# Two transformer blocks on one core: four of nine modulation groups summed on VectorE beside the input projections

## The chip, the core and the metric

The kernel runs on one NeuronCore of one Trainium2 chip. The core's engines have a queue of instructions each and wait for one another by semaphores: TensorE (PE; its weight loads are PEld) multiplies matrices into eight PSUM banks, VectorE (DVE) and ScalarE (ACT) read PSUM and on-chip memory, GpSimd (POOL) on-chip memory alone, and SyncE (SP) issues the transfers from main memory, which 16 engines carry out. The metric is the time of one execution on the device, in microseconds.

## The reference

The input is one sequence of 256 tokens of width 1024, in float32. The first block has two layers (l = 0 "even", l = 1 "odd"), the second block one more. What matters here is the modulation, a product of one vector with a wide matrix for each layer, which does not depend on the tokens:

```python
cs = silu(c)                                   # (1, 1024)
for l in range(2):
    mod = (cs @ ada_w[l] + ada_b[l])           # 1024 -> 6 x 1024
    sh1, sc1, g1, sh2, sc2, g2 = split(mod, 6)
    h = rms_norm(x, norm1_g[l]) * (1 + sc1) + sh1
    y = mixer_l(h, ...)                        # h @ w_in, rope, attention, @ w_out
    x = x + g1 * y
    h = rms_norm(x, norm2_g[l]) * (1 + sc2) + sh2
    x = x + g2 * hier_moe(h, ...)
```

The even mixer projects h to 3072 columns and has eight plain heads and four differential ones; the odd mixer projects to 2608 columns (five tiles of 512 and a tail of 48) and has 16 heads with two softmax branches and a third over compressed keys. Sixteen routed experts follow each.

## The kernel before, in words

**Weights.** All weights go through a ring of six slots (`ring`), each a tile of 1024 x 512 float32 (2 MB, 128 partitions x 8 chunks x 512). SP loads the tiles in the one order of the table `PHASES`; tile n goes into slot n mod 6 once TensorE has counted tile n - 6 as used (`tile_used`). An engine that reads a tile waits for `landed` of its slot.

**Modulation.** The vector of 2048 numbers of a group G is four tiles. Groups 0 to 2 belong to layer 0, 3 to 5 to layer 1 and 6 to 8 to the second block: 0, 3 and 6 hold shift and scale ahead of a mixer or an expert stage that has to wait for them, and 1, 2, 4, 5 are wanted only later (gate 1, shift 2, scale 2, gate 2). `mod_tile` takes a tile in 32 matmuls: for each of 8 chunks and 4 quarters q of the columns the stationary operand is one column of `cact` spread over 32 columns, and the moving one the 128 columns of the weight; the result is on rows 32 q of a bank. A float32 matmul leaves two records in the trace, so a tile is 64. ScalarE copies the bank (`mod_out`), TensorE turns it in four transposes (`mod_turn`), and VectorE adds the bias and makes 1 + scale (`mod_columns`), which raises `mod_ready`.

**Where it stood.** Groups 1, 2 (layer 0) and 4, 5 (layer 1) were spread over the steps of the attentions `att0` and `att1` by `mod_chunk_steps`: a tile per step in `att0`, a third of a tile per step in `att1`. Their bank 2 and copy in `hT` are free there.

**Attention.** `att0` has eight items, `att1` 24 (eight rounds of two plain items and a compressed one). In step t TensorE makes the scores of item t in banks 6 and 7 (L2178, L2180), then modulation, P times V of item t - 1 - lag (L2202), and the transposes of P of item t - lag (L2227). VectorE in step t copies its half of the turned P (L543), makes the masked maximum of the scores of t (L1334), and normalises item t - 1 by the sums of the exponentials (L1344 to L1363); ScalarE copies its half, makes the exponentials of t (L931) and copies an output out (L938). lag is 1 in `att0` and 2 in `att1`. Scores of t + 1 wait for the maximum of t.

**Input projections.** `project` takes a weight tile in 2 x 8 matmuls of 128x512 (L2117), a row of tokens after another, into two of the four banks 0 to 3. Between the halves stand transposes of q and k by groups (`BETWEEN`; L2072), which alternate between banks 4 and 5: group g waits until g - 2 has been copied out, even ones by ScalarE (L1092), odd ones by VectorE (L1801). VectorE's and ScalarE's loops over the tiles j first copy the groups up to the first half of tile j, then tile j's result to `pb`. GpSimd applies the rope in between. In layer 1 VectorE makes, after the groups of j = 4, eight adds (L1845) for the compressed keys, which the matmuls of L2751 need.

## Time and profile before

| | us |
|---|---|
| median of 3 runs | 1359.21 (1359.13 to 1361.91) |
| profiled execution | 1359.62, its span 1357.9 |
| TensorE busy, share of the span | 1232.0, 91% |
| VectorE busy | 444.3, 33% |
| ScalarE, GpSimd busy | 267.6 and 115.8 |
| moved from main memory | 355.14 MB, 262 GB/s over the span |
| L2135, the modulation's matmuls, all nine groups | 82.1 in 2304 records |

The span's start is zero in all views. A stretch's line gives each engine's busy time in it; busy times count a pipelined matmul to its modelled end, so that those of neighbours overlap by some 0.1 us. PEclk is the clock that TensorE was granted as a share of 2.4 GHz; 0.50 is its lower level of 1.2 GHz. What stands in brackets after an instruction is its engine's idle time before it and who ended it. The first input projection runs from 36 to 125 us, `att0` to 163, the second projection from 357 to 433, `att1` from 456 to 533.

### The profile page before, as it was taken

Reading aid. Unit: us, or ns where it says so; the run is one execution under the profiler, and the core shown is the slowest. Engines: PE = TensorE matmul, PEld = TensorE weight load, DVE = VectorE, ACT = ScalarE, POOL = GpSimd, SP = SyncE. Lnnn points to the kernel's source line nnn. Section 1 sums busy time; section 2 is a strip of 40 time slices with the busy share of each in tenths; the row PEclk is TensorE's granted clock in tenths of the full one; section 3 lists DMA queues with packets and bytes.
Section 4 is the critical chain, followed back from the end, with each engine's and each line's share of the span. In section 5 each row is a group of like instructions: output and inputs, shape, how many; then the busy total and the mean of one; then the engine's idle time right before and its main releaser. Section 6 shows DMA issues by size and latency. Waiting matters only on the chain.

```text
span 1357.9 us, 17790 instructions
## 1 busy us (share of the span) xinstructions
PE 1232.0 (91%) x7440; PEld 649.5 (48%) x7440; DVE 444.3 (33%) x1148; ACT 267.6 (20%) x621; POOL 115.8 (9%) x202
## 2 busy tenths in 40 slices
PE   4999987999799899799999999899999599999895
PEld 4445743435445665344448845555545343333332
DVE  1102643113203574421153642431132731201124
ACT  0102511122101354212112122002320311020010
POOL 1010010000011000100001000000000222222221
PEclk9899997999999799989999999999999799999998
DMA  9956964999983565469999533383326579999993
GB/s 355 369 177 205 368 202 141 348 373 387 384 291 124 205 233 184 139 211 348 380 386 387 210 124 124 124 300 136 114 101 216 218 253 362 382 387 387 386 385 122
DMA packets 222955, 357.43 MB, mean 263 GB/s; under 512 B 15845, under 2 KB 86038, under 8 KB 222870
## 3 DMA queue, kind: packets, MB, share of 16 engines
q1 hardware_dynamic: 209056, 352.33, 73.6%
q10 hardware_dynamic: 13814, 3.87, 1.3%
q8 instruction: 64, 1.05, 0.3%
q14 instruction: 21, 0.17, 0.0%
HBM read 355.14 MB, written 1.05 MB: 262 GB/s over the span
## 4 chain that ended last, share of the span: by engine, by line
PE 82%; DVE 7%; DMA 4%; ACT 3%; issue 2%; SPq 1%; POOL 0%; DVEq 0%; ACTq 0%
PE bank L2117 20%; PE bank L2318 8%; PE bank L2524 8%; PE bank L2367 4%; PE bank L2810 4%; PE bank L2210 4%; PE bank L2135 4%; DMA ring<-in_w_down 3%; PE bank L2859 3%; PE bank L2293 3%; PE bank L2596 2%; PE bank L2387 2%; PE bank L2202 2%; PE bank L2227 1%; PE bank L2475 1%
## 5 line engine op out<-in xcount | busy, mean ns | idle before, releaser
L2117 PE MATMUL bank<-ring,hT 128*128 128x512 f32 x416 | 183.8, 601 | 3.3 <-ACT hT L895 2.4
L2117 PEld LDWEIGHTS bank<-ring,hT 128*128 128x128 f32 x416 | 79.2, 193 | 99.4 <-issue 98.6
L2524 PE MATMUL bank<-ring,A 128*64 128x512 f32 x512 | 116.5, 601 | 1.8 <-DVE pb L1722 1.8
L2318 PE MATMUL bank<-ring,A 128*64 128x512 f32 x512 | 117.2, 603 | 0.0
L2135 PE MATMUL bank<-ring,cact 128*32 128x128 f32 x2304 | 82.1, 297 | 18.0 <-issue 10.4
L2117 PE MATMUL bank<-ring,OT 128*128 128x512 f32 x224 | 97.2, 593 | 1.3 <-ACT OT L1212 0.8
L751 POOL TENSOR_TENSOR rstd<-rstd,nhalf 128x1 f32<-128x1 f32 x20 | 17.2, 859 | 810.2 <-DVE rstd L1281 810.2
L2135 PEld LDWEIGHTS bank<-ring,cact 128*32 128x32 f32 x2304 | 68.3, 119 | 33.4 <-issue 25.8
L2524 PEld LDWEIGHTS bank<-ring,A 128*64 128x64 f32 x512 | 35.1, 138 | 72.2 <-issue 70.7
L2117 PEld LDWEIGHTS bank<-ring,OT 128*128 128x128 f32 x224 | 42.2, 190 | 53.5 <-issue 52.5
L2318 PEld LDWEIGHTS bank<-ring,A 128*64 128x64 f32 x512 | 34.5, 138 | 66.6 <-issue 66.6
L2367 PE MATMUL bank<-ring,pb 128*64 128x512 f32 x256 | 57.0, 595 | 0.0
L2210 PE MATMUL bank<-ring,hT 128*128 128x512 f32 x128 | 55.8, 594 | 0.0
L2810 PE MATMUL bank<-hT,ring 128*128 128x256 f32 x256 | 55.8, 380 | 0.0
L2810 PEld LDWEIGHTS bank<-hT,ring 128*128 128x128 f32 x256 | 48.5, 190 | 6.7 <-issue 0.2
L2859 PE MATMUL bank<-ring,hT 128*128 128x512 f32 x96 | 42.2, 592 | 0.0
L2210 PEld LDWEIGHTS bank<-ring,hT 128*128 128x128 f32 x128 | 24.2, 190 | 29.1 <-issue 29.0
L543 DVE COPY PT<-bank 128x384 f32<-128x384 f32 (+1 forms) x34 | 17.7, 522 | 53.2 <-PE bank L2227 51.0
L1525 DVE TENSOR_TENSOR A_parts<-bank,OT_parts 128x512 fp32r<-128x512 f32 x32 | 22.1, 692 | 36.7 <-ACT OT_parts L1005 36.7
L2367 PEld LDWEIGHTS bank<-ring,pb 128*64 128x64 f32 x256 | 17.6, 137 | 34.5 <-issue 31.6
L2596 PE MATMUL bank<-ring,pb 128*64 128x512 f32 x128 | 29.0, 598 | 4.7 <-DMA ring<-in_w_down 4.7
L2293 PE MATMUL bank<-pb_parts 128*128 128x512 f32 x64 | 29.1, 455 | 3.7 <-DVE pb_parts L1458 3.7
(470 smaller groups left out, 1663.5 us busy)
## 6 DMA issues: line engine op xcount, KB each, us to landing
ring<-in_ada_w SPq DMA_DIRECT2D x24, 2048.0 KB, 10.1
ring<-in_moe_w_gate SPq DMA_DIRECT2D x32, 1024.0 KB, 8.0
ring<-in_moe_w_up SPq DMA_DIRECT2D x32, 1024.0 KB, 10.6
ring<-in_moe_w_down SPq DMA_DIRECT2D x16, 2048.0 KB, 19.7
ring<-in_w_gate SPq DMA_DIRECT2D x16, 2048.0 KB, 11.6
ring<-in_w_up SPq DMA_DIRECT2D x16, 2048.0 KB, 11.0
ring<-in_w_down SPq DMA_DIRECT2D x16, 2048.0 KB, 20.1
ring<-in_w_in SPq DMA_DIRECT2D x13, 2048.0 KB, 19.6
```

Of the source, the lines that this page charges most:

```text
L2117: ins = mm(B[2 * (m % 2) + tt][:], lhs[:, c, tt * P:(tt + 1) * P], w[:, c, :], start=c == 0, stop=c == C - 1)
L2135: ins = mm(B[MOD_RAW_BANK[G]][32 * q:32 * (q + 1), k * P:(k + 1) * P], cact[:, c0 + c:c0 + c + 1].broadcast_to([P, 32]), w[:, c, q * P:(q ...
L2202: ins = mm(dst, lhs, rhs, start=start, stop=stop)
L2210: ins = mm(B[2 + tt][:], hT[:, c, tt * P:(tt + 1) * P], w[:, c, :], start=c == 0, stop=c == C - 1)
L2293: ins = mm(bank[:], part[:, tt, c * P:(c + 1) * P], wide_sel[:, tt, 512 * half:512 * (half + 1)], start=tt + l == 0, stop=tt + l == 2)
L2318: ins = mm(B[r][64 * b:64 * (b + 1), :], wide_h[c][:, slot:slot + 64], w[:, 2 * r + b, :], start=c == 0, stop=c == C - 1)
L2367: ins = mm(B[r][64 * b:64 * (b + 1), :], hidT_small[half][k][:, slot:slot + 64], w[:, 2 * r + b, :], start=k == 0, stop=k == 1)
L2387: ins = mm(B[5 - j + tt][:], wT[NR * half + r][:, P * tt:P * (tt + 1)], part[r], start=half + r + l == 0, stop=half == 1 and r + l == NR)
L2524: ins = mm(B[r][64 * b:64 * (b + 1), :], wide_h[c][:, slot:slot + 64], w[:, 2 * r + b, :], start=c == 0, stop=c == C - 1)
L2596: ins = mm(B[r][64 * b:64 * (b + 1), :], hidT_wide[half][k][:, slot:slot + 64], w[:, 2 * r + b, :], start=k == 0, stop=k == 3)
L2810: ins = mm(B[2 * (m % 2) + a // 2][:, (a % 2) * T:(a % 2 + 1) * T], w[:, c, a * P:(a + 1) * P], hT[:, c, :], start=c == 0, stop=c == C - 1)
L2859: ins = mm(B[4 + q % 2][:], hT[:, c, (q % 2) * P:(q % 2 + 1) * P], w[:, c, :], start=c == 0, stop=c == C - 1)
```

## The change

Tiles of groups 1, 2, 4 and 5 are loaded between the tiles of the input projection of their layer. VectorE multiplies each chunk of such a tile by its column of `cact` and adds the eight up in half of `tmp` (`mod_sum`: one multiply, seven multiply-adds of 128x512); TensorE multiplies the sum with a stationary operand of 32 columns of ones, four matmuls in place of 32, behind the matmuls of a projection tile (`mod_summed_tile`). Copy, turn and columns move to the projection too, through banks 6 and 7 and the buffer `PT`. The attention's steps hold none of it any more. The tiles of the compression, `cmp`, are loaded behind the mixed ones. The functions `mod_chunk_steps` and `mod_group_step` go.

```diff
+EVIN = [("evin", 0), ("mod_b", 0), ("evin", 1), ("mod_b", 1), ("mod_b", 2), ("evin", 2), ("mod_b", 3), ("evin", 3),
+        ("mod_b", 4), ("mod_b", 5), ("evin", 4), ("mod_b", 6), ("mod_b", 7), ("evin", 5)]
+ODIN = [("odin", 0), ("mod_c", 0), ("odin", 1), ("mod_c", 1), ("mod_c", 2), ("odin", 2), ("mod_c", 3), ("mod_c", 4),
+        ("odin", 3), ("mod_c", 5), ("mod_c", 6), ("odin", 4), ("mod_c", 7)]
...
+SUMMED = {1: 0, 2: 4, 4: 8, 5: 12}
...
+        def mod_sum(G, k):
+            n, order = mod_tile_of(G, k), SUMMED[G] + k
+            acc = tmp[:, order % 2, :]
+            w = ring[n % NSLOT][:].rearrange("p (c n) -> p c n", n=512)
+            dve.wait_ge(landed[n % NSLOT], LANDED[n])
+            if order >= 2:
+                tile_ready(dve, mod_tile_of(*SUM_TILES[order - 2]))
+            step(v.tensor_scalar(acc, w[:, 0, :], cact[:, 0:1], None, ALU.mult))
+            for c in range(1, C):
+                ins = v.scalar_tensor_tensor(acc, w[:, c, :], cact[:, c:c + 1], acc, ALU.mult, ALU.add)
+                if c < C - 1:
+                    step(ins)
+            ins.then_inc(s["mod_summed"], 1)
...
         for j in range(6):
+            for G, k in (((1, 0),), ((1, 1), (1, 2)), ((1, 3),), ((2, 0), (2, 1)), ((2, 2), (2, 3)), ())[j]:
+                mod_sum(G, k)
             trans_out("qk0", to_A, groups=groups_in("evin", j))
             proj_out("evin", j, to_pb)
+            if j == 3:
+                mod_columns(1)
+        mod_columns(2)
         trans_out("qk0", to_A, groups=(6, 7))
...
         for j in range(5):
+            for G, k in (((4, 0),), ((4, 1), (4, 2)), ((4, 3), (5, 0)), ((5, 1), (5, 2)), ((5, 3),))[j]:
+                mod_sum(G, k)
             trans_out("qkv1", to_A, groups=groups_in("odin", j))
...
+        def mod_summed_tile(G, k):
+            if k == 0:
+                pe.wait_ge(s["mod_raw_out"], G)
+            pe.wait_ge(s["mod_summed"], SUMMED[G] + k + 1)
+            acc = tmp[:, (SUMMED[G] + k) % 2, :]
+            for q in range(4):
+                ins = mm(B[MOD_RAW_BANK[G]][32 * q:32 * (q + 1), k * P:(k + 1) * P], tri_one[:, P:P + 32],
+                         acc[:, q * P:(q + 1) * P], start=True, stop=True)
+            ins.then_inc(tile_used, 1)
...
-                G = mod_group_step(name, t, 1)
-                if G is not None:
-                    mod_turn(G)
-                for step in mod_chunk_steps(name, t):
-                    mod_tile(*step)
...
+        def odin_mod(j):
+            if j == 3:
+                mod_turn(4)
+            for G, k in (((4, 0),), ((4, 1), (4, 2)), ((4, 3), (5, 0)), ((5, 1), (5, 2)), ((5, 3),))[j]:
+                mod_summed_tile(G, k)
+        project("odin", 5, hT, turned="h2", between=qkv_group, after=odin_mod)
...
         ins.then_inc(s["tail_ready"], 1)
+        mod_turn(5)
```

`evin_mod` does the same for layer 0, with the lists of VectorE's loop; after the projection stands `mod_turn(2)`, and TensorE waits for `mod_ready` 3 before `att0`.

VectorE's queue in the second input projection, j = 1 to 4. L1801 (after: L1806) copies a transposed group into A, L530 and L535 (after: L515 and L520) a projected tile into `pb`. Before:

```order
L1835 COPY pb<-bank3 128x512
L1801 COPY A<-bank5 128x512
L530 COPY pb<-bank1 128x512 x2
L1801 COPY A<-bank5 128x512 x2
L530 COPY pb<-bank3 128x512
L535 COPY pb<-bank3 128x256
L1801 COPY A<-bank5 128x512
L1854 MEMSET OT 32x256
L1845 TENSOR_TENSOR pb<-A,cols 64x480 x8
```

The same place after, from j = 2:

```order
L515 COPY pb<-bank1 128x512 x2
L1319 TENSOR_SCALAR tmp<-ring3,cact 128x512
L1321 SCALAR_TENSOR_TENSOR tmp<-ring3,cact,tmp 128x512 x7
L1319 TENSOR_SCALAR tmp<-ring4,cact 128x512
L1321 SCALAR_TENSOR_TENSOR tmp<-ring4,cact,tmp 128x512 x7
L1806 COPY A<-bank5 128x512 x2
L515 COPY pb<-bank3 128x512
L520 COPY pb<-bank3 128x256
L1300 TENSOR_TENSOR modc<-bank6,cols 128x16
```

Between tile 2's copy and the copies of groups 3 and 5 (the x2) stand now the sums of two tiles, in the ring's slots 3 and 4.

TensorE's queue in `att0`, the steps t = 1 and 2, before:

```order
L2178 MATMUL bank7<-A 128x128
L2180 MATMUL bank6<-A 128x256
L2180 MATMUL bank7<-A 128x256
L2135 MATMUL bank2<-ring5,cact 32x128 x32
L2227 MATMUL bank4<-ident,tmp 128x128 x3
L2227 MATMUL bank5<-ident,tmp 128x128 x3
```

And after:

```order
L2204 MATMUL bank7<-A 128x128
L2206 MATMUL bank6<-A 128x256
L2206 MATMUL bank7<-A 128x256
L2248 MATMUL bank4<-ident,tmp 128x128 x3
L2248 MATMUL bank5<-ident,tmp 128x128 x3
```

The 32 matmuls of a tile are gone from between scores and transposes; nothing else changed its place there.

## Rows read from the trace of the kernel before

**Rows 1.** Stretch, length, then busy us per engine, PEclk, DMA share, GB/s.

```profile
36.00:125.00 89.00, 89.00 (x224) 40.79 (x224) 7.21 (x13) 6.45 (x14) 9.48 (x20) 0.97 0.73 235
125.90:163.10 37.20, 35.11 (x676) 27.41 (x677) 24.71 (x113) 21.40 (x81) 0.00 (x0) 1.00 1.06 375
...
456.00:532.60 76.60, 70.34 (x936) 46.21 (x936) 55.48 (x229) 42.22 (x162) 0.00 (x0) 0.96 0.67 220
```

**Rows 2.** The same for line L2135 alone, in the two attention stretches.

```profile
125.90:163.10 37.20, 15.78 (x512) 13.61 (x512) 1.00 1.06 375
456.00:532.60 76.60, 19.80 (x512) 13.30 (x512) 0.96 0.67 220
```

**Rows 3.** TensorE in time, first attention: start, us, operation, idle before.

```profile
125.97 0.49 PE L2178 MATMUL bank<-A 64*128 64x128 f32 x4 [0.83 <-DVE A L1801]
...
126.82 1.95 PE L2135 MATMUL bank<-ring,cact 128*32 128x128 f32 x64
128.71 0.49 PE L2178 MATMUL bank<-A 64*128 64x128 f32 x4
...
132.18 0.84 PE L2227 MATMUL bank<-ident,tmp 128*128 128x128 f32 x6 [0.66 <-DVE tmp L1363]
132.95 0.49 PE L2178 MATMUL bank<-A 64*128 64x128 f32 x4
...
137.30 0.49 PE L2178 MATMUL bank<-A 64*128 64x128 f32 x4
...
146.88 0.66 PE L2147 MATMUL bank<-ident,hT 128*128 128x128 f32 x4
```

**Rows 4.** VectorE in time, same place.

```profile
125.17 0.69 DVE L1801 COPY A<-bank 128x512 f32<-128x512 f32 x1 [0.18 <-PE bank L2072]
...
129.68 0.29 DVE L1334 CUSTOM_DVE_ANT_0 Pm<-bank,mask 128x128 f32<-128x128 f32 x1 [1.18 <-PE bank L2180]
...
131.00 1.02 DVE L1363 TENSOR_TENSOR tmp<-tmp,rr 128x256 f32<-128x256 f32 x2
```

**Rows 5.** TensorE in time, one round of the second attention.

```profile
482.40 0.49 PE L2178 MATMUL bank<-A 64*128 64x128 f32 x4
...
489.90 0.65 PE L2202 MATMUL bank<-PT,vcmp 15*64 15x256 f32 x4 [0.45 <-ACT PT L543]
...
491.28 0.49 PE L2178 MATMUL bank<-A 64*128 64x128 f32 x4
```

**Rows 6.** ScalarE in time, the same round.

```profile
487.64 0.40 ACT L931 ACTIVATE Pm<-Pm,nmx 128x128 f32<-128x128 f32 x1 [0.54 <-DVE nmx L1334]
...
489.41 0.34 ACT L543 COPY PT<-bank 15x256 f32<-15x256 f32 x1
```

**Rows 7.** TensorE in time, second input projection.

```profile
357.23 34.57 PE L2117 MATMUL bank<-ring,hT 128*128 128x512 f32 x80 [0.68 <-DVE hT L1255]
...
407.12 1.04 PE L2072 MATMUL bank<-ident,pb 128*128 128x128 f32 x8
...
433.07 7.12 PE L2751 MATMUL bank<-ring,pb 128*60 128x256 f32 x64
```

**Rows 8.** VectorE in time, second input projection.

```profile
400.79 0.68 DVE L1801 COPY A<-bank 128x512 f32<-128x512 f32 x1
...
417.17 7.92 DVE L1845 TENSOR_TENSOR pb<-A,cols 64x480 f32<-64x480 f32 x8
```

**Rows 9.** Busy time by stretch: the transfers of the second input projection.

```profile
357.00:375.00 18.00, 17.77 (x42) 7.99 (x43) 2.05 (x6) 1.93 (x5) 2.37 (x5) 1.00 1.05 382
```

**Rows 10.** One group of VectorE instructions: count, busy us, mean ns.

```profile
L1747 DVE SCALAR_TENSOR_TENSOR x<-x,Pm 128x512 f32<-128x512 f32 x8 | 5.5, 692 | 0.3
```

**Rows 11.** Busy time by stretch: where the granted clock is low.

```profile
204.00:213.00 9.00, 1.46 (x6) 1.36 (x6) 6.97 (x30) 2.30 (x4) 2.35 (x1) 0.61 0.00 0
...
440.00:445.00 5.00, 2.93 (x22) 2.19 (x21) 2.23 (x4) 2.37 (x5) 0.00 (x0) 0.99 0.74 234
445.00:461.00 16.00, 14.17 (x124) 11.91 (x127) 5.67 (x21) 4.06 (x11) 0.00 (x0) 0.50 0.51 190
```

More of the change, by code:

```diff
@@ L580, in columns, with mixed @@
                      w.rearrange("(c p) n -> p c n", p=P)[:, :, col0 + 512 * j:col0 + 512 * (j + 1)])
+        def mixed(phase, sources):
+            for name, j in phase:
+                w, col0 = sources[name]
+                n = TILE_NO[name, j]
+                load(n, n % NSLOT, kview(n % NSLOT),
+                     w.rearrange("(c p) n -> p c n", p=P)[:, :, col0 + 512 * j:col0 + 512 * (j + 1)])
         def moe_small(name, wg, wu, wd):
@@ L648, in _ @@
         columns(p["ada_w"][1], TILE["mod_h2"], 0, 4)
-        columns(p["od_w_in"][0], TILE["odin"], 0, 5)
+        mixed(ODIN, {"odin": (p["od_w_in"][0], 0), "mod_c": (p["ada_w"][1], 2048)})
         for j in range(2):
@@ L2104, in bank_pair_free, with project @@
                 proj_evacuated(pe, m - 2)
-        def project(name, tiles, lhs, first=0, turned=None, between=None):
+        def project(name, tiles, lhs, first=0, turned=None, between=None, after=None):
             for j in range(first, tiles):
@@ L2124, in project, with mod_tile @@
                         between(g)
-        def mod_tile(G, k, chunks=range(C)):
-            if k == 0 and chunks[0] == 0 and G:
+                if after is not None:
+                    after(j)
+        def mod_tile(G, k):
+            if k == 0 and G:
                 pe.wait_ge(s["mod_raw_out"], G)
@@ L2132, in mod_tile @@
             c0 = C if G >= 6 else 0
-            for c in chunks:
+            for c in range(C):
                 for q in range(4):
@@ L2696, in qk_group, with evin_mod @@
             transposes("qk0", from_tokens(pb, lambda c: P * c if c < 8 else 1536 + P * (c - 8)), [g])
-        project("evin", 6, hT, turned="h0", between=qk_group)
+        def evin_mod(j):
+            if j == 3:
+                mod_turn(1)
+            for G, k in (((1, 0),), ((1, 1), (1, 2)), ((1, 3),), ((2, 0), (2, 1)), ((2, 2), (2, 3)), ())[j]:
+                mod_summed_tile(G, k)
+        project("evin", 6, hT, turned="h0", between=qk_group, after=evin_mod)
+        mod_turn(2)
         stage_transposed(pe, "qk0")
+        pe.wait_ge(s["mod_ready"], 3)
         proj_evacuated(pe, PROJ["evin"] + 5)
```

84 lines of the change are left out of this document (34 added, 50 removed).

## The prediction

> **What bounds the kernel now.** I first read the busy time by stretch [rows 1]. In the first input projection (36 to 125 us) TensorE is busy all the 89 us while VectorE has 7.2 and the transfer engines 0.73 of their time: room for sums. In the first attention TensorE is busy 35.1 of 37.2 us and in the second 70.3 of 76.6, so both look bound by TensorE too, and the modulation line L2135 has 15.8 and 19.8 us of that [rows 2], 16 tiles of about 1.9 us at full clock. The temptation is to count 30 us as the gain. The view in order of time says otherwise, and it is the one that decides: the reader should follow one step of each attention from matmul to matmul and ask what would be late if the modulation matmuls were not there.
>
> **First attention.** In the step that starts at 128.71 TensorE has already no P times V to do, and it idles 0.66 us for VectorE: start 128.71, next start 132.95, 4.24 us [rows 3]. Its inside: scores, VectorE's masked maximum from 129.68, reciprocal, the normalising multiply from 131.00 for 1.02 us [rows 4], then TensorE's six transposes from 132.18 until 132.95 [rows 3]. Scores of item t, maximum of t, normalising of t-1 and transposes of t-1 stand in this order on two in-order queues, so they are a loop that no other instruction shortens. The fuller step from 132.95 to 137.30 takes 4.35 us [rows 3]. Taking its modulation tile away gives 4.24, not 4.35 - 1.9: 0.1 us. So I cost it: three plain steps 0.1 each, the first step 0.45 (2.74 from 125.97 to 128.71 [rows 3]; without the tile, 0.97 until VectorE starts, as from 128.71 to 129.68 [rows 3, 4], and 1.3 for the maximum up to the normalising at 131.00, 2.3), the step with the turn 0.1. Together -0.9 us. Bounds: 0 to -15.8, the whole of L2135 there [rows 2]; I take the value of the step that idles, since it is the same work.
>
> **Second attention.** A round is three items: 482.40 to 491.28, 8.88 us [rows 5]. It holds one tile, 1.9 us, and 0.45 us in which TensorE waits at 489.90 for ScalarE's copy of P [rows 5]. That copy stands behind the round's second exponentials (487.64 to 489.41 [rows 6]), these behind VectorE's maximum, this behind the second scores. Before those scores stand 16 of a tile's 64 records, 0.5 us; without them ScalarE starts its exponentials 0.5 earlier, and no more, since it has the previous item's copy to make until then. The other 48 records of the round stand at places where TensorE would wait for ScalarE instead. So a round loses about 0.54: 8.34. Seven rounds give -3.8 us; the first is held by VectorE's compressed softmax and gives nothing. Bounds: 0 and -19.8 [rows 2].
>
> **What the input projections get.** TensorE: per tile four matmuls, 8 records of the 64 of a tile: 0.24 us, 2.0 per layer. The turn of a group (four transposes) took 0.66 at 146.88 [rows 3], some 0.6 net; inside an attention it partly filled waits, now it stands in line. VectorE: per tile one multiply and seven multiply-adds over 128x512. The trace has this shape from on-chip memory at 692 ns [rows 10]; with 0.03 for the step between dependent instructions 0.72, and the first about 0.5: 5.5 us a tile. Bounds per instruction: 0.69, the bare row, to 1.0, the mean of the eight adds that take 7.92 at 417.17 [rows 8].
>
> First projection: five pairs or singles of sums, at most 11 us, stand ahead of VectorE's copies of a tile that takes 13.7 us on TensorE, and of evacuations needed only later; at j = 3 and 4 they end some 2 us before TensorE wants them. Hidden, if 0.72 holds. In line on TensorE: 2.0 + 0.6 (turn of group 1) = +2.5. At the end, VectorE now has group 2's columns ahead of its last copy into A, and these wait for the turn: before, copy at 125.17 and scores at 125.97 [rows 3, 4]; now turn 0.6 and three small instructions 0.4 in between: +1.0. First half: +2.5 + 1.0 - 0.9 = +2.6.
>
> Second projection: here is the term that sets my forecast. TensorE starts at 357.23 [rows 7] as soon as its first tile has landed, with no stock: the previous stage has emptied the ring, and the transfers run at 382 GB/s with no pause [rows 9]. A tile of 2.097 MB takes 5.49 us, so tile i behind the first lands at about 357 + 5.49 i. Before, the five weight tiles were next to each other and far ahead of use. Now the order is w0 m0 w1 m1 m2 w2 m3 m4 w3 m5 m6 w4 m7. m5 (i = 9) lands at 406.4, m6 (i = 10) at 411.9. VectorE sums them one after the other (411.9, then 417.4), and only then makes the copy of transposed group 3 into A, which before it made at 400.79 [rows 8]. Group 5 uses the same bank as group 3, so TensorE, which transposed groups 4 and 5 at 407.12 [rows 7] (5 from 407.56), waits in the middle of weight tile 3, with half of it, tile 4 and the tail queued behind. It goes on at 417.4 + 0.7 = 418.1: +10.5 us against 407.56; the multiplies that TensorE got earlier in this stage (1.2 us for five tiles) run inside that. After it: turn of group 4 0.6, two tiles 0.5, the last tile 0.24, turn of group 5 0.6: +1.95 before the compression matmuls of 433.07 [rows 7]. VectorE's last sum (m7, lands at 423) and its eight adds of 7.9 end near 441, about when TensorE is through tile 4; just hidden. w2 and w3 land at 384.5 and 401, each within a us of their use.
>
> Clock. A 9 us stretch with TensorE busy 1.46 has a mean grant of 0.61, so it fell to 1.2 GHz inside [rows 11]; the stall above is 8 to 9 us long, so it falls there too. The grant of 0.97 over 89 us of dense work after a pause [rows 1] is 5.3 us at half clock, which costs 2.7; I take +2.4 (0 to 3). The second attention already begins at 1.2 GHz: 0.50 from 445 to 461, full soon after with TensorE busy 14.2 of 16 [rows 11]. Without modulation matmuls the filling is thinner and recovery later, at the first dense steps: four pieces of 0.8 more at half clock, less what waits hide: +2.4 (0 to 5).
>
> Sum: 2.6 + 10.5 + 1.95 + 2.4 + 2.4 - 3.8 = +16.1. The profiled execution took 1359.6 (span 1357.9), the median is 1359.2: 1375.3 us. Later stages start with a full ring as before and only shift. Registers, semaphores and issues on SP stay as many; its loads are the same in another order.
>
> **A rule against the change.** The busy time falls to about 2.5 of 4.24 us per step in the first attention. From 440 to 445 TensorE was busy 2.93 of 5 us, and from 445 the grant is 0.50, until 461 [rows 11]. The Trainium skill, TensorE: Matmul & The Clock Gate, section "A second HAM failure mode: psum-queue depth-cycling", says that many short idles between groups of matmuls can make the clock oscillate without one long gap. By that rule, the fall after 440 to 445 agrees, and the first attention would swing; no other stretch here shows it. That is rival 2 below, priced there from rows.
>
> **Rivals.**
> 1. Attention is TensorE's after all: faster. If the vector chain shrinks with less queueing, the 15.8 + 15 us of tiles at full clock come back; with the rest of the sum (2.6 + 0.9, 10.5, 1.95, 2.4) that is 1359.2 + 18.4 - 30.8 = 1346.8; without the stall 1335. It decides once a step of the first attention goes under about 3.5 us. Against: the step at 128.71, which idles with no more than this work. Chance 0.06.
> 2. The clock falls inside the attentions. At half clock scores and transposes double on the loop: 0.85 (125.97 to 126.82) + 0.77 (132.18 to 132.95 [rows 3]) = 1.6 us on each of 8 steps, 13 us if all of the first, 6 if half; 1359.2 + 16.1 + 6 = 1381, at most about 1390. For: the fall at 445. Against: over the dense attention before, the grant is 1.00. Chance 0.17.
> 3. No stall: the sums take so little or the loads come so early that group 3 is copied in time. Then 10.5 shrinks to the 1.2 of inserted multiplies and the clock term after it goes: 1359.2 + 2.6 + 1.2 + 1.95 + 2.4 - 3.8 = 1363.6. With the second clock term gone too, 1362. Against: m6's landing alone is at 411.9. Chance 0.14; of this 0.04 within 0.2%.
> 4. VectorE cannot keep up: 1.0 us per multiply-add, 7.7 a tile, 15.4 per pair against 13.7 of a weight tile. Then the first projection stalls too, by some 2 at j = 3 and 4 each, and the second by 4.4 more: 1384. GpSimd's rope may add to it. Chance 0.08.
> The forecast itself has 0.55.
>
> **Range and chances.** 1364 to 1387. Under 0.2% (2.7 us) nothing can be told from no change: faster 0.06, within 0.04, slower 0.90.
>
> **What would show it.** Right: TensorE idle 7 to 10 us before a transposition in weight tile 3 of the second projection, released by VectorE's copy; VectorE's multiply-adds near 0.7; steps of 4.24 and rounds of 8.3 us; no idle in the first projection above 0.5. Wrong: attention steps near 2.5 us, a copy of group 3 before 408, or a low clock in the first attention.

## The result and the profile after

The changed kernel took 1396.72 us (median of 4 runs, 1391.71 to 1401.52) against 1359.24 (1359.13 to 1361.91) for the kernel before: ratio 1.0265, 95% interval 1.0240 to 1.0291. Slower was forecast; the amount was not: 1375.3 us, with a range that ended at 1387. The profiled execution took 1392.90 us with a span of 1391.2, so the two profiles have 33.3 us between them. The four executions differ by 10 us where the kernel before differs by 3, and the longer ones had the lower mean clock: 1391.7, 1392.9, 1400.5 and 1401.5 us at 0.948, 0.943, 0.937 and 0.934.

Where the 33.3 us arise, by the first matmul of each stage in the two timelines ("places" are the matmuls behind the choice of experts):

| stretch | before | after | difference | forecast |
|---|---|---|---|---|
| start to first scores of `att0` | 125.97 | 130.67 | +4.70 | +3.5 |
| `att0` | 37.15 | 41.42 | +4.27 | -0.9 |
| gate spread to the places of the first expert stage | 47.23 | 48.72 | +1.49 | 0 |
| from there to the second projection | 146.88 | 150.88 | +4.00 | 0 |
| second projection | 75.84 | 88.57 | +12.73 | +14.85 |
| compression | 23.02 | 22.86 | -0.16 | 0 |
| `att1` | 76.54 | 80.43 | +3.89 | -1.4 |
| gate spread to the end | | | +2.4 | 0 |

The stretches of the changed kernel that answer to [rows 1]; in a line stand busy time and instructions of PE, PEld, DVE, ACT and POOL, then the granted clock, the share of the transfer engines and GB/s:

```profile
38.00:128.00 90.00, 90.00 (x284) 40.82 (x283) 52.51 (x74) 5.66 (x10) 12.54 (x20) 0.98 1.09 360
130.67:172.09 41.42, 27.33 (x156) 18.54 (x157) 24.26 (x108) 19.62 (x78) 0.00 (x0) 0.71 0.44 139
483.12:563.55 80.43, 59.46 (x417) 37.15 (x417) 55.39 (x223) 41.10 (x160) 0.00 (x0) 0.83 0.01 1
```

VectorE's 52.5 busy us in the first projection, 45 more than in [rows 1], cost TensorE no wait there. Both attentions have less work and take longer, and what stands out is the clock: 0.71 and 0.83, where [rows 1] have 1.00 and TensorE was busy 35.1 of 37.2 us. One step of the first attention at each level, in TensorE's timeline, is the picture to keep:

```profile
137.92 0.80 PE L2204 MATMUL bank<-A 64*128 64x128 f32 x4
138.51 1.06 PE L2206 MATMUL bank<-A 64*128 64x256 f32 x4
139.50 1.55 PE L2223 MATMUL bank<-PT,pb 128*64 128x256 f32 x8
142.12 0.84 PE L2248 MATMUL bank<-ident,Pm 128*128 128x128 f32 x6 [1.07 <-DVE Pm L1371]
142.89 0.49 PE L2204 MATMUL bank<-A 64*128 64x128 f32 x4
143.22 0.60 PE L2206 MATMUL bank<-A 64*128 64x256 f32 x4
143.75 0.87 PE L2223 MATMUL bank<-PT,pb 128*64 128x256 f32 x8
146.37 0.85 PE L2248 MATMUL bank<-ident,tmp 128*128 128x128 f32 x6 [1.75 <-DVE tmp L1371]
147.14 0.49 PE L2204 MATMUL bank<-A 64*128 64x128 f32 x4
```

The same four scores take 0.80 in the first step and 0.49 in the second. The full-clock step is 147.14 - 142.89 = 4.25 us (forecast 4.24), the slow one 4.97. In place of the modulation tile TensorE now idles 1.1 to 1.8 us ahead of the transposes. The clock falls and comes back every step or two, all through the attention.

The stall of the second projection, on TensorE and on VectorE, is at the forecast place; before, the same copies followed each other as in [rows 8], and [rows 7] show group 5 without a wait:

```profile
424.59 0.60 PE L2087 MATMUL bank<-ident,pb 128*128 128x128 f32 x4
430.47 1.08 PE L2087 MATMUL bank<-ident,pb 128*128 128x128 f32 x4 [5.27 <-DVE A L1806]
431.35 8.66 PE L2132 MATMUL bank<-ring,hT 128*128 128x512 f32 x16
```
```profile
417.24 0.57 DVE L1319 TENSOR_SCALAR tmp<-ring,cact 128x512 f32<-128x512 f32 x1 [0.59 <-DMA ring<-in_ada_w]
417.84 5.97 DVE L1321 SCALAR_TENSOR_TENSOR tmp<-ring,cact,tmp 128x512 f32<-128x512 f32 x7
423.73 0.48 DVE L1319 TENSOR_SCALAR tmp<-ring,cact 128x512 f32<-128x512 f32 x1
424.24 5.47 DVE L1321 SCALAR_TENSOR_TENSOR tmp<-ring,cact,tmp 128x512 f32<-128x512 f32 x7
429.64 0.68 DVE L1806 COPY A<-bank 128x512 f32<-128x512 f32 x1
```

The copy of group 3 stands behind two sums, and the half tile after it begins at half clock (8.66 us for 16 records that take 7.1 at full clock; mean grant 0.80 from 431 to 440 us). The first of the two sums waits for its tile, m5 by the prediction's name, to land; the second, m6's, follows it at once.

What nobody had forecast is in the modulation of group 3, which the change does not touch. The kernel before first, then the changed one:

```profile
339.56 1.17 PE L2135 MATMUL bank<-ring,cact 128*32 128x128 f32 x33
344.42 3.70 PE L2135 MATMUL bank<-ring,cact 128*32 128x128 f32 x128 [3.69 <-issue]
350.63 2.82 PE L2135 MATMUL bank<-ring,cact 128*32 128x128 f32 x95 [2.51 <-issue]
```
```profile
354.86 5.16 PE L2151 MATMUL bank<-ring,cact 128*32 128x128 f32 x97 [4.89 <-issue]
360.64 3.70 PE L2151 MATMUL bank<-ring,cact 128*32 128x128 f32 x128 [0.63 <-issue]
366.84 1.08 PE L2151 MATMUL bank<-ring,cact 128*32 128x128 f32 x31 [2.50 <-issue]
```

TensorE stands still with no semaphore to wait for, and the pieces are 33, 128, 95 records before and 97, 128, 31 after: in both kernels two interruptions are 128 records apart, and they have moved by 64. The changed kernel has a third and longest wait, 4.89 us, ahead of the first record of the group; it comes in every trace whose first such edge is at record 97, and why it stands there, and not 128 records ahead of the edge, is open.

### The profile page after: what moved, and what is told of

It reads as the page before. It is cut to its first block, busy times and chain, and to the rows that moved or that the text cites. A ratio compares the mean times of both kernels' runs of the same rounds, so it can differ in the third digit from the quotient of the medians.

```text
span 1391.2 us, 16140 instructions
## 1 busy us (share of the span) xinstructions
PE 1230.1 (88%) x6544; PEld 641.1 (46%) x6544; DVE 539.5 (39%) x1276; ACT 267.5 (19%) x621; POOL 121.9 (9%) x202
## 4 chain that ended last, share of the span: by engine, by line
PE 78%; DVE 9%; DMA 7%; ACT 3%; issue 3%; SPq 1%; DVEq 0%; POOL 0%; ACTq 0%
PE bank L2132 18%; PE bank L2339 8%; PE bank L2545 7%; DMA ring<-in_w_down 4%; PE bank L2388 4%; PE bank L2849 4%; PE bank L2231 4%; PE bank L2898 3%; PE bank L2151 3%; PE bank L2314 3%; DMA ring<-in_ada_w 3%; PE bank L2408 2%; PE bank L2617 2%; PE bank L2248 2%; PE bank L2496 1%
## 5 line engine op out<-in xcount | busy, mean ns | idle before, releaser
L2132 PE MATMUL bank<-ring,hT 128*128 128x512 f32 x416 | 187.1, 607 | 3.3 <-ACT hT L886 2.4
L1321 DVE SCALAR_TENSOR_TENSOR tmp<-ring,cact,tmp 128x512 f32<-128x512 f32 x112 | 88.0, 786 | 4.0
L742 POOL TENSOR_TENSOR rstd<-rstd,nhalf 128x1 f32<-128x1 f32 x20 | 17.2, 858 | 814.8 <-DVE rstd L1274 814.8
L2132 PEld LDWEIGHTS bank<-ring,OT 128*128 128x128 f32 x224 | 42.2, 190 | 53.5 <-issue 52.5
L2151 PE MATMUL bank<-ring,cact 128*32 128x128 f32 x1280 | 48.6, 319 | 19.3 <-issue 12.5
L2388 PE MATMUL bank<-ring,pb 128*64 128x512 f32 x256 | 57.0, 595 | 0.0
L2231 PE MATMUL bank<-ring,hT 128*128 128x512 f32 x128 | 55.8, 594 | 0.0
L2151 PEld LDWEIGHTS bank<-ring,cact 128*32 128x32 f32 x1280 | 43.7, 130 | 24.4 <-issue 18.3
L2898 PE MATMUL bank<-ring,hT 128*128 128x512 f32 x96 | 42.2, 592 | 0.0
L1501 DVE TENSOR_SCALAR A<-bank,modc 128x512 f32<-128x512 f32 x16 | 13.0, 810 | 58.7 <-PE bank L2314 58.7
L2388 PEld LDWEIGHTS bank<-ring,pb 128*64 128x64 f32 x256 | 17.6, 137 | 34.5 <-issue 33.3
```

What stands on the lines that cost most here:

```text
L1321: ins = v.scalar_tensor_tensor(acc, w[:, c, :], cact[:, c:c + 1], acc, ALU.mult, ALU.add)
L2132: ins = mm(B[2 * (m % 2) + tt][:], lhs[:, c, tt * P:(tt + 1) * P], w[:, c, :], start=c == 0, stop=c == C - 1)
L2151: ins = mm(B[MOD_RAW_BANK[G]][32 * q:32 * (q + 1), k * P:(k + 1) * P], cact[:, c0 + c:c0 + c + 1].broadcast_to([P, 32]), w[:, c, q * P:(q ...
L2231: ins = mm(B[2 + tt][:], hT[:, c, tt * P:(tt + 1) * P], w[:, c, :], start=c == 0, stop=c == C - 1)
L2388: ins = mm(B[r][64 * b:64 * (b + 1), :], hidT_small[half][k][:, slot:slot + 64], w[:, 2 * r + b, :], start=k == 0, stop=k == 1)
L2898: ins = mm(B[4 + q % 2][:], hT[:, c, (q % 2) * P:(q % 2 + 1) * P], w[:, c, :], start=c == 0, stop=c == C - 1)
```

## Experiments

Each ran 4 to 12 times, beside the kernel before on the same chip. The kernel before has another median on each chip: 1359.0 us for fill_both, thin_before, sum_order and fill_sum_order; 1362.1 for pad_before, pad_before_16, pad_change and half_fill; 1358.0 for best_change, quarter_fill, warm_experts and warm_more; 1361.2 for wide_fill, warm_all, warm_compression and changed_warm. Its single executions there spread over 7 to 10 us. So times of different groups are to be compared by their ratios. Lengths of stretches come from the one profiled execution of each; "clock" is the granted clock over the attention. First theories: **T1**, the attentions lose time because TensorE's clock falls without the filler; **T2**, VectorE's order makes the stall. **T3** came with the first traces: the "issue" waits belong to blocks of the instruction stream.

| kernel | median us | ratio to before, 95% | `att0`, clock | `att1`, clock | second projection |
|---|---|---|---|---|---|
| before | 1359.2 | 1 | 37.15, 1.00 | 76.54, 0.96 | 75.84 |
| changed | 1396.7 | 1.0240-1.0291 | 41.42, 0.71 | 80.43, 0.83 | 88.57 |
| fill_both | 1382.0 | 1.0141-1.0196 | 37.80, 1.00 | 76.28, 0.96 | 88.72 |
| thin_before | 1368.2 | 1.0042-1.0079 | 39.01, 0.87 | 74.94, 0.91 | 75.84 |
| sum_order | 1384.7 | 1.0155-1.0201 | 41.30, 0.71 | 84.61, 0.78 | 81.07 |
| fill_sum_order | 1376.2 | 1.0098-1.0142 | 37.70, 1.00 | 76.27, 0.96 | 81.61 |
| half_fill | 1376.0 | 1.0092-1.0121 | 36.29, 1.00 | 76.43, 0.92 | 81.07 |
| wide_fill | 1374.0 | 1.0079-1.0129 | 37.11, 1.00 | 77.96, 0.96 | 81.06 |
| best_change | 1369.9 | 1.0061-1.0109 | 36.30, 1.00 | 78.38, 0.90 | 81.07 |
| quarter_fill | 1381.1 | 1.0134-1.0185 | 39.48, 0.83 | 87.35, 0.79 | 81.63 |
| pad_change | 1372.8 | 1.0058-1.0085 | 37.78, 1.00 | 76.27, 0.96 | 81.81 |
| pad_before | 1366.3 | 1.0016-1.0046 | 37.44, 1.00 | 76.55, 0.96 | 75.84 |
| pad_before_16 | 1366.8 | 1.0022-1.0048 | 37.14, 1.00 | 76.54, 0.96 | 75.84 |
| changed_warm | 1365.0 | 1.0017-1.0055 | 37.32, 0.96 | 74.96, 0.96 | 81.42 |

### Is it the clock in the attentions?

**fill_both**, the changed kernel with

```diff
+                for c in fill_chunks(name, t):     # att0: all 8; att1: a third of 8 per step
+                    for q in range(4):
+                        mm(B[2][32 * q:32 * (q + 1), 0:P], cact[:, c:c + 1].broadcast_to([P, 32]), ident[:],
+                           start=True, stop=True)
```

> The changed kernel with matmuls that compute nothing put back where the modulation matmuls stood in both attentions: 32 of the same shape in each of the eight steps of the first, a third of a tile in each step of the second, on data that is resident and into bank 2, which nobody reads. Theory (T1): the attentions lost time only because TensorE's clock fell to its lower level once the filler was gone. Then the grant is 1.0 in the first attention and in most of the second, steps take 4.35 instead of 4.25 and 4.96, rounds 8.9 instead of 8.3 and 9.9, and the gate's spread 1.95 instead of 3.43; the first attention gets 4.5 us shorter and the second about 3.5, so 1396.7 - 8 = 1388.7, although TensorE does some 30 us of work more. Rival: the attentions are slower because something on VectorE's or ScalarE's side takes longer (memory shared with GpSimd, a later start), and the clock only goes along: then more work on TensorE gives nothing back or costs, 1396 to 1400. Side question: this kernel has again nearly as many TensorE instructions ahead of the modulation of group 3 as before; if the 'issue' waits there depend on the position in the instruction stream, they change back from 8.0 to about 6.2 us; if they depend on the transfers, they stay.

Measured 1382.0: some 30 us of useless work on TensorE (8 times 1.95 us and 24 thirds of it) made the kernel 14.7 us faster (8 expected by the profile's stretches; the profiled execution of the changed kernel was one of its two short ones). `att0` is back to 37.80 at 1.00 and `att1` to 76.28 at 0.96. The rival of a slower vector chain falls. So does one that was not named, that the attention suffers from the thinner transfers: `att0` has them at 375 GB/s before and at 139 after, but fill_both has 161 there and the full clock, and thin_before, below, has 374 and a clock that falls. The side question got no answer here: the "issue" waits stayed as in the changed kernel, which both of its theories allow, as the counts below show.

**thin_before**, the kernel before with

```diff
             for c in chunks:
                 for q in range(4):
+                    if G in (1, 2, 4, 5) and c != C - 1:
+                        continue
...
```

> The kernel before, in which the modulation of groups 1, 2, 4 and 5 leaves out seven of the eight chunks of each tile, so that those values are incomplete; 4 of 32 matmuls of each tile stay, in the attentions, and nothing moves to the projections. It is the removal alone, without the sums. T1: the clock falls in the attentions as it does after the change: steps near 4.96 at half clock and 4.25 at full clock in turn, the first attention some 3 to 4 us longer than before and the second some 2 to 4, so 1359.2 + 6 = 1365, up to 1368 with what follows. Prediction as recorded (the attention terms -0.9 and -3.8, no clock): 1354.5. Rival 1 of the prediction (TensorE bounds the attentions): 1359.2 - 28/32 * 30 = 1333.

1368.2 us: removing 28 of 32 matmuls of 16 tiles, which leaves seven eighths of each sum out, costs 0.42 to 0.79%. The first scores of three successive steps of `att0`, in TensorE's timeline, stand at half clock and then at full clock, as after the change:

```profile
133.32 0.80 PE L2180 MATMUL bank<-A 64*128 64x128 f32 x4
...
138.29 0.49 PE L2180 MATMUL bank<-A 64*128 64x128 f32 x4
...
142.54 0.49 PE L2180 MATMUL bank<-A 64*128 64x128 f32 x4
```

4.97 us, then 4.25. `att1` gains 1.6. Of the loss, `att0` has 1.9, and the modulation of group 3 has 4.6 (below), which the expectation had not counted; the trace is 4.5 us late at the gate spread behind `att1`, and what it loses later was not followed up. So the forecast total was met by luck: the two attentions together lost 0.3 us where 5 to 8 were expected, and the edge of the instruction blocks made up for it. What the run shows of T1 is the clock, 0.87 and 0.91, and the swing of the steps. Both the recorded 1354.5 and rival 1's 1333 are excluded.

**half_fill** (16 matmuls a step in `att0`, 5 chunks of four in three steps of `att1`), **quarter_fill** (8, and 4 in each) and **wide_fill** are the changed kernel with VectorE's order of the next section and another filler. quarter_fill and wide_fill also have useless matmuls ahead of the expert stages (32, 0 and 16, 8; see below), which put the edge back to record 33. wide_fill has

```diff
+                for n in {"att0": (512, 512) if t < 8 else (), "att1": (384,) if t < 24 else ()}.get(name, ()):
+                    mm(B[2][:, 0:n], ident[:], bc(ident[:], 1, [P, n // P, P]), start=True, stop=True)
```

> The changed kernel with VectorE's divided order and half of the filler: 16 matmuls in each step of the first attention, 5 chunks of four in three steps of the second where there were 8. The count of records stays the same modulo 128. If half is enough to keep the clock, steps are 4.25 to 4.35 us, a round 8.5, the time is 1375 to 1376, like the whole filler. If not, steps alternate between 4.25 and 4.96 as without filler, and the time is 1380 to 1385 (1384.7 without any).

> As best_change, with a quarter of the filler: 8 matmuls in each step of the first attention, one chunk of four in each of the second. 4 per step (the kernel before with one chunk in eight) was too little, 16 is enough. If the clock holds: the time of best_change within 1 us. If it falls in some steps, each costs 0.7 us, rounds up to 1.5: 2 to 8 us more.

> As fill_sum_order with the edges put back, but the filler is two matmuls of 128x128 by 512 columns in a step of the first attention (4 records instead of 64, 1.76 us instead of 1.9) and one of 384 in each of the second. If the clock follows the time that TensorE is busy, attentions are as with the whole filler: 1370 to 1373. If it follows the number of matmuls or of weight loads, it falls as without filler: 1378 to 1381.

The stretch of `att0` in half_fill, quarter_fill and wide_fill (the granted clock is the number ahead of the last two):

```profile
129.50:165.80 36.30, 27.14 (x412) 19.44 (x413) 24.25 (x108) 19.49 (x78) 0.00 (x0) 1.00 0.53 170
```
```profile
129.40:168.90 39.50, 28.40 (x285) 18.99 (x285) 24.27 (x108) 19.58 (x78) 0.00 (x0) 0.83 0.50 157
```
```profile
130.50:167.60 37.10, 33.79 (x188) 18.50 (x189) 24.27 (x108) 19.50 (x78) 0.00 (x0) 1.00 0.50 157
```

Half keeps the clock in `att0` and a quarter does not; quarter_fill costs 11 us against best_change, its sibling with half, more than the 2 to 8 expected, nine of them in `att1` (87.35 against 78.38). Four long records a step keep the clock as 64 short ones do (37.11 us at 1.00 against 37.78 at 1.00 in pad_change, which has the whole filler and the same edge), so the count of matmuls is not what decides here. And half_fill, whose filler fits into TensorE's idle time, shows the step without the tiles once the clock holds: 36.29 against 37.15, that is -0.86 us, the -0.9 of the prediction.

### Is it VectorE's order?

**sum_order**, and **fill_sum_order** with the filler of fill_both as well:

```diff
-            for G, k in (...)[j]:
-                mod_sum(G, k)
-            trans_out("qkv1", to_A, groups=groups_in("odin", j))
+            sums = (...)[j]
+            trans_out("qkv1", to_A, groups=BETWEEN["odin"].get((j - 1, 1), ()))
+            for G, k in sums[:1]:
+                mod_sum(G, k)
+            trans_out("qkv1", to_A, groups=BETWEEN["odin"].get((j, 0), ()))
+            for G, k in sums[1:]:
+                mod_sum(G, k)
```

> The changed kernel; only VectorE's order in the second projection differs: the copy of the groups that are transposed behind the previous tile comes first, then the first sum, then the copy of the groups transposed in the middle of this tile, then the second sum. T2: the stall of 8 to 10 us in weight tile 3 stood behind the order. Group 3 is then copied near the time of before, group 5 behind the sum of m5 and without a wait for m6; TensorE waits only for the sum of m6, 2 to 3 us, and perhaps 1 to 2 before the compression. So 12.7 shrinks to about 5 and the slow stretch behind the stall (1.6) goes: 1396.7 - 8 = 1388.7. Rival: the stage is bound by the landings of thirteen mixed tiles, and m6's landing holds whoever wants it: then only 1 to 2 us come back, 1395.

> Both edits together, the filler matmuls in both attentions and the divided order of VectorE in the second projection. If T1 and T2 are separate mechanisms the gains add: 1396.7 - 16 = 1381. If one is the other's cause (the clock of the second attention falls because of the stall ahead of it), the sum is smaller than its parts by 2 us or more: 1384 or above.

The stage shrinks from 88.57 to 81.07 us, and in TensorE's timeline of sum_order the group after the first half of weight tile 3 follows at once; only ScalarE's copy of the modulation's row is waited for:

```profile
418.43 0.43 PE L2167 MATMUL bank<-tmp,tri_one 128*32 128x128 f32 x8
419.56 0.43 PE L2167 MATMUL bank<-tmp,tri_one 128*32 128x128 f32 x8 [0.70 <-ACT PT L863]
419.91 7.13 PE L2136 MATMUL bank<-ring,hT 128*128 128x512 f32 x16
426.88 1.04 PE L2091 MATMUL bank<-ident,pb 128*128 128x128 f32 x8
427.76 7.03 PE L2136 MATMUL bank<-ring,hT 128*128 128x512 f32 x16
```

T2 holds: 1384.7, not the 1395 of a stage bound by landings, and the 2 to 3 us that m6 was still to cost did not come. What is left, 5.2 us over the kernel before, is this 0.7 and, for the most part, the inserted work. The two gains, 14.7 and 12.0, add to 26.7, but together they give 20.5: fill_sum_order took 1376.2, less than either of the two times written ahead, and the gains fall short of their sum by 6. By the expectation's own rule that speaks for a link between the two; none was shown. What the traces show is that the unfilled `att1` is not the same from kernel to kernel (80.43 us in one trace, 84.61 in the other, and 76.27 and 76.28 in both filled ones), so that the filler's share has no fixed size.

### What are the waits without a semaphore?

In all six traces then known the edges fell at record 33 (before) or 97 (all others) of group 3. The page's lines on instruction counts and on the queue that brings instructions, before and after:

```profile
PE 1232.0 (91%) x7440; PEld 649.5 (48%) x7440; DVE 444.3 (33%) x1148; ACT 267.6 (20%) x621; POOL 115.8 (9%) x202
...
q8 instruction: 64, 1.05, 0.3%
```
```profile
PE 1230.1 (88%) x6544; PEld 641.1 (46%) x6544; DVE 539.5 (39%) x1276; ACT 267.5 (19%) x621; POOL 121.9 (9%) x202
...
q8 instruction: 57, 0.93, 0.3%
```

To move the edge alone, TensorE gets useless matmuls where it waits 6.5 us anyway, n = 32, 32 in **pad_before**, 16, 4 in **pad_before_16**; **pad_change** is fill_sum_order with 32, 32, **best_change** half_fill with 32, 0:

```diff
         def places(i):
+            for q in range(n[i]):
+                mm(B[3][32 * (q % 4):32 * (q % 4 + 1), 0:P], cact[:, 0:1].broadcast_to([P, 32]), ident[:],
+                   start=True, stop=True)
             pe.wait_ge(s["chosen_ready"], i + 1)
```

> The kernel before with 32 matmuls that compute nothing (128x32, resident data, into bank 3) ahead of TensorE's longest wait in each of the first two expert stages, where it idles 6.5 us anyway. In all traces so far the 'issue' waits in the modulation of groups 3 and 6 stand 128 records apart, and in group 3 at record 33 in the kernel before but at record 97 in the five others, whose count of TensorE records ahead of that place differs by -448 or +64, both 64 modulo 128. Theory (T3): the wait belongs to a block of 128 records of TensorE's instruction stream, and where the block's edge falls in the group sets the price. Then the pads move the first edge from 33 to 97 (the two pads together move group 6 by 128, nothing), the stretch from the first expert stage's wait to the second projection gets 4 us longer, 146.9 to 150.9, and the time is 1363. Rival: the waits follow from what the transfers are doing, and the shift in the changed kernel from its later start: then nothing moves and the time stays 1359.0.

> The kernel before with 16 and 4 such matmuls instead of 32 and 32. By T3 the edges move to record 1 of group 3 and to record 0 of group 6. The price of a position in between is not known; if it falls from 97 (8.0 us of waits) over 33 (6.2) further to 1, the first wait shrinks by another 1 to 2 us in each group, since it starts earlier, and the time is about 1356. If the rival holds, 1359.0. If the wait at the edge is a constant one whatever is ahead of it, 1359 to 1361.

> The changed kernel with filler in both attentions and VectorE's divided order (1376.2 us), and the two pads of 32 on top. By T3 the first edge in group 3 goes back from record 97 to 33 and 4 us come back: 1372. By the rival nothing: 1376.

> The changed kernel with all that helped so far: half of the filler in the attentions, VectorE's divided order, and 32 matmuls ahead of the first expert stage's long wait, which put the first edge back to record 33 in group 3 and to record 40 in group 6. If the three mechanisms (clock, order, edge of the instruction blocks) are all there is besides the work added in the projections, it gains on half_fill (1376.0) the 4 us of group 3 and some 2 of group 6: 1370. The kernel before stays ahead by the added 4 us of the first and 6 us of the second projection. Rival: something unnamed is left, and the time is 1374 or above.

Group 3 in TensorE's timeline of pad_before:

```profile
344.26 5.06 PE L2135 MATMUL bank<-ring,cact 128*32 128x128 f32 x97 [4.87 <-issue]
349.91 3.70 PE L2135 MATMUL bank<-ring,cact 128*32 128x128 f32 x128 [0.59 <-issue]
356.11 1.08 PE L2135 MATMUL bank<-ring,cact 128*32 128x128 f32 x31 [2.50 <-issue]
```

The picture of the changed kernel, in the kernel before: 150.66 us for the stretch in place of 146.88, and 1366.3 against 1362.1 (ratio 1.0016 to 1.0046). pad_change gets them back: 146.91 us, and a ratio of 1.0058 to 1.0085 against the 1.0098 to 1.0142 of fill_sum_order. best_change has 145.81 in place of half_fill's 151.42. Its 1369.9 is the 1370 that was expected, but on a chip with a faster kernel before: the ratio 1.0061 to 1.0109 overlaps half_fill's 1.0092 to 1.0121, so the gain at the end is not shown there. T3 holds for the place of the waits, and its rival, waits made by the state of the transfers, falls as the cause of the shift. But the transfers decide whether there are such waits at all. Two other dense runs of the same matmuls in the kernel before, with the transfers at 146 and 267 GB/s and not at 386, have none:

```profile
885.53 8.67 PE L2135 MATMUL bank<-ring,cact 128*32 128x128 f32 x256
1037.01 5.96 PE L2135 MATMUL bank<-ring,cact 128*32 128x128 f32 x192
```

pad_before_16 missed: with the edge at record 1 the stretch took 148.80, and the kernel was 0.22 to 0.48% slower, where I had expected 1356. The price does not fall steadily with the edge's place; of the three places tried, 33 was the best.

### The same theory turned round

If useless matmuls keep the clock, they should speed up the kernel before where it is slow: behind the long wait ahead of each expert stage, and in the compression. **warm_experts** puts 64 matmuls of 192 columns ahead of each stage, all into rows 0 to 31 of the bank; **warm_more** has 64, 60 and 64, and also four matmuls of 256 or 512 columns in short waits of the compression; **warm_all** is the same, but uses the four quarters of the rows in turn; **warm_compression** has the four alone; **changed_warm** is half_fill with the four and with 96, 60 and 64 matmuls of 128 columns ahead of the stages.

```diff
+        def warm(n, cols, bank=3):
+            for i in range(n):
+                q = 32 * (i % 4)               # warm_experts, warm_more: q = 0
+                mm(B[bank][q:q + 32, 0:cols], cact[:, 0:1].broadcast_to([P, 32]),
+                   bc(ident[:, 0:64], 1, [P, cols // 64, 64]), start=True, stop=True)
```

> The kernel before with 64 matmuls of 128x32 by 192 columns, which compute nothing, ahead of TensorE's longest wait in each of the three expert stages (6.5, 6.5 and 6.1 us, after which the clock is at its lower level for some 9 us in the trace of before). The clock theory (T1) turned round: if a stretch of idle costs the clock and useless matmuls keep it, then filling the wait gives back the slow stretch behind it: some 8 us of work at half clock are 4 us each where TensorE bounds what follows, at most 12 in all, less what the transfers then hold back: 1350 to 1357 against 1359 to 1362 for the kernel before. Rival: the wait is on VectorE's chain and the stages behind it are bound by the weights' transfers: nothing, or 1 to 2 us worse where the filler overruns the wait. The edges of the instruction blocks stay where they are.

> As warm_experts, and one useless matmul each of 256 or 512 columns in four short waits (1.2, 0.55, 0.6 and 0.94 us) between the compression and the second attention, where the clock of the kernel before falls at 444 us and stays low until 461. If the clock needs little more than it has there, the 17 us at half clock are full and TensorE gets 3 to 6 us back: 1346 to 1354. If the narrow matmuls of that stretch (15 to 64 columns) are what lets it fall, nothing changes or it costs 1: as warm_experts.

> As warm_more, but the 64 matmuls ahead of each expert stage's long wait go to four quarters of the bank's rows in turn, as the modulation's do. In warm_experts all went to one quarter and took 0.164 us a record, 21.0 us for 64 matmuls of 192 columns; the modulation's take 0.029 us a record of 128 columns. If the quarters are what lets them overlap, 64 take 5.6 us and fit in the wait of 6.5. The stretch behind the first wait was 1.9 us shorter with a full clock (144.95 against 146.88 us to the second projection), and the one from compression to the second attention 4.3 shorter (18.7 against 23.0). So 4.3 + 1.9 + about as much again for the two other expert stages: 1358 - 8 to 10 = 1348 to 1350, faster than the kernel before. Rival: what TensorE gains in the expert stages is taken by the weights' transfers: only the 4.3 stay, 1354.

> The kernel before with only the four useless matmuls between compression and second attention. The clock's share alone: 4.3 us off that stretch, 1358 - 4.3 = 1353.7. The second attention itself starts at the lower clock as before in both. Rival: the earlier second attention meets a later landed weight and gives it back: 1358.

> The changed kernel with half filler and divided order (half_fill), plus the same useless matmuls in the waits (96, 60 and 64 of 128 columns ahead of the expert stages, which keep the edges at record 33 and 40, and the four in the compression). Does keeping the clock close the distance to the kernel before? The gains are of the same places in both, so best_change minus 8: 1369.9 - 8 = 1362, and the distance to warm_all stays 12, the work and waits that the sums add to the projections. If the distance shrinks by more than 4, the clock is part of those too.

warm_experts took 1405.7 us and warm_more 1400.2 (ratios 1.0316 to 1.0364 and 1.0275 to 1.0325), since the filler takes nearly four times as long as I had thought. Its line in warm_experts, then in warm_all:

```profile
203.52 20.99 PE L2264 MATMUL bank<-ident,cact 128*32 128x192 f32 x128
```
```profile
203.56 7.09 PE L2265 MATMUL bank<-ident,cact 128*32 128x192 f32 x128
```

The local effects came: the compression took 18.59 us at clock 1.00 in warm_all (23.02 at 0.76 before), and the stretch from the first expert stage to the second projection 145.00 (146.88). At the gate spread behind `att1` warm_all is 6.15 us ahead. Yet the kernel took 1360.3 us (ratio 0.9983 to 1.0014), warm_compression 1360.4 (0.9985 to 1.0017): no gain that can be measured. In warm_all's trace the lead was lost piece by piece: the clock fell elsewhere (0.70 against 0.88 from 865 to 893 us, about 3 us), the third expert stage's pad, 8.07 us at a grant of 0.66, overran its wait (about 2), and the rest went in the last stage, for a reason that was not followed up. My expectation of 1348 to 1350 added local gains as if nothing behind them could answer. changed_warm took 1365.0 (1.0017 to 1.0055), the best form of the change: it is 4.8 us behind warm_all, not 12, so by what was written ahead the clock has a part in that distance too; which part was not followed up. No version was faster than the kernel before.

## Why the prediction was wrong, step by step

- **Start to `att0`, +3.5: nearly right, +4.70.** The last transposes of the first projection come 3.86 us later (+2.5 forecast): a single summed tile costs 0.36 and not 0.24 on TensorE; the tiles and the turn together take 2.96, and the last 0.9 was not followed up. From those transposes to the scores it is 0.84 us more than before, where 1.0 had been put.
- **VectorE's price, a little low.** 112 multiply-adds have a median of 752 ns and a mean of 786 (0.72 taken from [rows 10], 0.69 to 1.0 as bounds), and the first projection does not stall. Rival 4 was wrong.
- **`att0` -0.9 and `att1` -3.8: the step that failed.** As work they are right: 4.25 us a step, and full-clock rounds such as 512.08 to 520.39 with 8.31 (8.34 forecast); half_fill has the -0.86. But they were priced at a clock that only the removed matmuls had kept; the +2.4 set beside them was for a later recovery at the start of `att1` alone. Measured +4.27, then +1.49 since the gate spread behind it runs at half clock (3.43 us in place of 1.95), and +3.89 instead of -1.4 in `att1`. This is 12.0 us of the 17.2 by which the sum was short. Rival 2 named this mechanism and priced `att0` at 6 us, but had chance 0.17, because [rows 1] show the attention dense at clock 1.00. That grant was measured with the filler in it: it could not speak for the state without it. The row that could was [rows 11], the thin stretch at 440 to 445 with the fall behind it. Here the rule of the Trainium skill that the prediction weighed (TensorE: Matmul & The Clock Gate, section "A second HAM failure mode: psum-queue depth-cycling"), many short idles between groups make the clock swing, agrees with the trace: 0.71 over steps whose idle is 1.1 to 1.8 us. How far it falls is not fixed by the change: `att1` took 74.94 us in thin_before, near the forecast -1.4, and 80.43 here; the -3.8 came out in single rounds only, in no whole `att1`.
- **Second projection, right in place and cause, and 2.1 too long.** The copy of group 3 behind m6's sum holds group 5. But the landing that counts is m5's, 45.6 us behind TensorE's start and not 49.2, with two sums behind it that take 12.5; m6's sum waited for no landing. And since TensorE came to group 4 3.0 us later than before and not 1.2, it idled 5.27 us, less than the 7 to 10 that were named as the sign. Of +12.45 of work and stall and +2.4 of clock, +12.73 came in all; the slow stretch behind the stall cost 1.6. sum_order took 7.5 of it away. The stall is no law of the sums but of the order in which two of them stand ahead of a copy.
- **Modulation of group 3, 0 forecast, +4.00.** "Registers, semaphores and issues stay as many" was said, and "later stages only shift". The count of matmuls was not considered as something that itself has a price at a distance: 448 records fewer move the edge of the instruction blocks. The waits grow from 6.20 to 8.02 us, and the rest is half clock behind the first one (5.16 us for 97 records, where 95 at full clock take 2.82). This is 4.0 of the 17.2.
- **After `att1`, +2.4:** 1.7 of it lies in the last expert stage between 1158.6 and 1211.0 us (52.4 us in place of 50.7). There 70 records that took 12.43 us without a pause take 14.13, and the grant is 0.88 in place of 1.00: the clock fell in the midst of dense work. Why was not tested.
- The median lies 4 us above the profiled execution; that the swing of the clock differs from run to run fits the four mean clocks, but the kernel before spread as widely on other chips. In rival 3, 1363.6 less the second clock term is 1361.2, not 1362. A range worked out from one trace has to be wider on the side where a swing can start.

## What to carry to other kernels

A matmul that costs nothing on the critical path may still be what keeps TensorE's clock; before moving it away, price the loop that stays at the lower level of the clock too, and take the granted clock of a dense stretch as evidence for that stretch only. Where small matmuls stand densely while the transfers run at full rate, a change in the number of TensorE instructions can move time hundreds of microseconds later, so compare the "issue" waits and their record counts before explaining such a shift by the stage it falls in. In an in-order queue, put a short copy that another engine waits for ahead of a long optional sum that has to wait for its data.

## What the hardware showed that was not expected

- With the transfer engines at 386 GB/s, a block of 128 matmul records came every 6.2 us (344.42 to 350.63, 360.64 to 366.84, 710.91 to 717.12 us), while TensorE runs 128 such records in 3.7 at full clock. At 146 and 267 GB/s, 256 and 192 records ran without such a wait (8.67 and 5.96 us). That the supply of instructions holds the dense run, and that the weight transfers slow it, is the reading that fits all traces; no run changed the transfers alone.
- Matmuls that fill 32 output rows and go to four quarters of the rows in turn take 0.111 us each at a mean grant of 0.76 (7.09 for 64 of 192 columns in warm_all) and 0.085 at 1.00 (5.08 for 60, its second stage); those that all go to one quarter take 0.328 at 1.00 (20.99 for 64 in warm_experts): nearly four times as long for the same work.
- The kernel before can be made faster for its first 530 us by useless matmuls (6 us) without being faster at its end.
